# Three weight slabs instead of two beside three of a transformer block's norms

## The reference

```python
h = rms_norm(x, norm_mix[l])
proj = h @ w_in[l]                 # pool, q, k, v, the inputs of a recurrent mixer, gates
...                                # three branches from it, merged under gates
x = x + merged @ w_out[l]
x = x + conv_glu_ffn(rms_norm(x, norm_ffn[l]), ffn_up[l], ffn_conv[l], ffn_down[l])
```

## Time and profile before

| | |
|---|---|
| median of 3 runs | 2850.2 us (2846.32 to 2850.47) |
| profiled execution, device time | 2849.13 us |
| its span in the trace | 2847.3 us |
| granted TensorE clock, mean | 0.981 of full |
| TensorE busy | 2722.3 us, 96% |
| VectorE, ScalarE busy | 1810.7 us, 1119.0 us |

### The profile page before, as it was taken

One profiled execution on the slowest core, in us unless ns is written; L12 is line 12 of the kernel. 1 busy time (PEld: TensorE's weight loads), 2 busy tenths in 40 slices (PEclk: granted clock), 3 DMA queues, 4 the chain that ended last, 5 costly groups with the idle time before them and its releaser, 6 DMA issues. The chain is left out here.

```text
span 2847.3 us, 59014 instructions
## 1 busy us (share of the span) xinstructions
PE 2722.3 (96%) x25807; PEld 2489.7 (87%) x25807; DVE 1810.7 (64%) x2741; ACT 1119.0 (39%) x1818; POOL 376.0 (13%) x223
## 2 busy tenths in 40 slices
PE   8999999999999999999999999999999999899997
PEld 7988998898999998988998898999887887777785
DVE  5744345555888645834345555888637985787786
ACT  6332324523333224423324523333323343366564
POOL 0310122130111100310122130111100000010001
PEclk9999999999999999999999999999999999799999
DMA  3211222364333342211322362333322212299996
GB/s 143 76 44 34 83 82 62 118 200 171 121 133 134 121 142 91 79 37 34 94 71 73 106 191 82 119 134 135 117 91 88 94 33 74 94 411 402 381 396 252
DMA packets 115355, 380.23 MB, mean 134 GB/s; under 512 B 12800, under 2 KB 13968, under 8 KB 114704
## 3 DMA queue, kind: packets, MB, share of 16 engines
q1 hardware_dynamic: 89712, 307.18, 31.4%
q10 hardware_dynamic: 17712, 41.36, 4.0%
q0 software_dynamic: 7664, 27.82, 2.6%
HBM read 340.17 MB, written 36.13 MB: 132 GB/s over the span
## 5 line engine op out<-in xcount | busy, mean ns | idle before, releaser
L307 PE MATMUL PS<-HR,HIGHR 128*128 128x264 f32 (+1 forms) x3008 | 856.7, 285 | 1.9 <-issue 1.9
L307 PE MATMUL PS<-XR,HIGHR 128*128 128x264 f32 (+2 forms) x1792 | 564.2, 315 | 15.5 <-DVE HR L431 9.8
L307 PEld LDWEIGHTS PS<-HR,HIGHR 128*128 128x128 f32 x3008 | 570.5, 190 | 5.1 <-issue 2.1
L307 PE MATMUL PS<-XR,RINGR 128*128 128x264 f32 (+1 forms) x1600 | 456.1, 285 | 0.0
L307 PE MATMUL PS<-HH,HIGHR 128*128 128x264 f32 (+2 forms) x1504 | 436.9, 290 | 10.5 <-ACT SMALL L388 5.7
L291 ACT CAST HIGHR<-RING 128x1024 fp32r<-128x1024 f32 (+2 forms) x340 | 330.7, 977 | 265.8 <-DMA RING<-wts 117.3
L307 PE MATMUL PS<-HH,RINGR 128*128 128x264 f32 (+2 forms) x1504 | 432.1, 287 | 0.0
L302 DVE TENSOR_TENSOR RINGR<-RING,HIGHR 128x1024 fp32r<-128x1024 f32 (+2 forms) x272 | 304.9, 1125 | 163.3 <-ACT HIGHR L291 150.4
L307 PEld LDWEIGHTS PS<-XR,HIGHR 128*128 128x128 f32 x1792 | 339.9, 190 | 42.1 <-issue 12.2
L307 PE MATMUL PS<-ARENA 64*64 64x64 f32 (+7 forms) x8890 | 332.4, 234 | 29.6 <-issue 15.7
L307 PEld LDWEIGHTS PS<-ARENA 64*64 64x64 f32 (+4 forms) x8890 | 286.0, 140 | 66.1 <-issue 21.5
(11 more groups left out here) (403 smaller groups left out, 4820.0 us busy)
## 6 DMA issues: line engine op xcount, KB each, us to landing
RING<-wts SPq DMA_DIRECT2D x324, 512.0 KB, 3.6
ARENA<-wmoe SPq DMA_DIRECT2D x210, 512.0 KB, 7.4
RING<-wts SPq DMA_DIRECT2D x52, 256.0 KB, 3.0
gates<-STAGE ACTq DMA_DIRECT2D x48, 264.0 KB, 4.3
ARENA<-gates ACTq DMA_DIRECT2D x48, 264.0 KB, 3.2
ys<-RING ACTq DMA_DIRECT2D x17, 512.0 KB, 6.8
ys<-STAGE POOLq DMA_DIRECT2D x15, 512.0 KB, 11.4
RING<-wts SPq DMA_DIRECT2D x16, 384.0 KB, 3.0
```

The lines of the kernel that those rows point to most:

```text
L307: return e.matmul(out, lhsT, rhs, start=start, stop=stop, skip_group_check=True)
```

## The change

Two constants are new: `LIN_BESIDE` gives the number of slabs side by side behind the mix norm of each layer (layer 0 keeps two, layer 1 has three), and `UP_BESIDE` lists the three up slabs side by side behind the ffn norm of both layers. The calls of `high_parts` and `low_parts` that stand ahead of the norm now reach one slab further. On ScalarE that call stands behind the last square and ahead of the norm's table load; on VectorE ahead of the first scaling. The calls behind the norm stay as they are, and so do slab order and banks.

```diff
+LIN_BESIDE = (2, 3)
+UP_BESIDE = [(0, 0), (0, 1), (1, 0)]
...
-    slabs = [slab(0), slab(1)]
-    two_at = [banks.place(w, (l, "in", i), 2) for i in range(2)]
-    two = project_beside(k, e, w, slabs, k.hx, lambda q: s["part_dve"][l, "h", q], two_at, cut=True)
+    first = [slab(i) for i in range(LIN_BESIDE[l])]
+    first_at = [banks.place(w, (l, "in", i), 2) for i in range(len(first))]
+    beside = project_beside(k, e, w, first, k.hx, lambda q: s["part_dve"][l, "h", q], first_at, cut=True)
     for i in range(14):
-        if i < 2:
-            two[i].then_inc(*P.done((l, "in", i)))
+        if i < len(first):
+            beside[i].then_inc(*P.done((l, "in", i)))
...
-    high_parts(k, e, w, k.slabs.index["lin", l, 1] + 1)
+    high_parts(k, e, w, k.slabs.index["lin", l, LIN_BESIDE[l] - 1] + 1)
     rms_act(k, e, w, ("mix", l), k.rs)
...
-    low_parts(k, e, w, "lo_dve", k.slabs.index["lin", l, 1] + 1)
+    low_parts(k, e, w, "lo_dve", k.slabs.index["lin", l, LIN_BESIDE[l] - 1] + 1)
...
         if f == 0:
-            slabs = [slab(0, p) for p in range(2)]
-            at = [banks.place(w, ("up", l, 0, p), 2) for p in range(2)]
-            two = project_beside(k, e, w, slabs, rhs, lambda q: s["part_dve"][l, "f", q], at, T - t0, cut=True)
+            first = [slab(*x) for x in UP_BESIDE]
+            at = [banks.place(w, ("up", l, *x), 2) for x in UP_BESIDE]
+            beside_of = dict(zip(UP_BESIDE, project_beside(k, e, w, first, rhs, lambda q: s["part_dve"][l, "f", q], at,
+                                                           T - t0, cut=True)))
         for p in range(2):
-            if f == 0:
-                two[p].then_inc(*s["up_pe"].done((l, f, p)))
+            if (f, p) in beside_of:
+                beside_of[f, p].then_inc(*s["up_pe"].done((l, f, p)))
...
-    high_parts(k, e, w, k.slabs.index["up", l, 0, 1] + 1)
+    high_parts(k, e, w, k.slabs.index["up", l, 1, 0] + 1)
     rms_act(k, e, w, ("ffn", l), k.rs)
...
-    low_parts(k, e, w, "lo_dve", k.slabs.index["up", l, 0, 1] + 1)
+    low_parts(k, e, w, "lo_dve", k.slabs.index["up", l, 1, 0] + 1)
```

## The result

The changed kernel takes 2856.24 us in the median of 11 runs (2853.02 to 2863.87), the kernel before 2850.69 in 11 runs beside it (2845.11 to 2852.68). The ratio is 1.0025, with a 95% interval from 1.0015 to 1.0035: slower by 4 to 10 us. The forecast was 5.1 us slower, a median of 2855.3 in a range from 2850.5 to 2860.5.

What follows compares the result with a forecast made beforehand. TensorE, busy 2722.3 of 2847.3 us, was taken as the bound. A loss of 1.8 us without the clock plus 3.3 from it made 5.1 slower: 2854.2 profiled, median 2855.3, range 2850.5 to 2860.5.

Steps and rivals of the forecast that it cites:

- The clock's term: Half-clock falls behind the new stalls: likeliest two of three stages, mix among them, 1.6 + 1.7 = 3.3 us lost.
- one sign that was named for being wrong: Across the three stages: the clock falling at none or all of them would show the prediction wrong.
- The split ahead of the norm: ScalarE's copy between last square and table load lengthens the norm by 0.9 us, 0.45 in layer 1's mix norm.
- Three slabs fill the gaps: Behind the norms TensorE runs 144 matmuls without a gap; three slabs end 3.6, 2.9 and 2.0 us earlier, 8.4 in sum.
- The stall ahead of (1,1): Up stages: TensorE idles some 2.7 us for (1,1)'s low part; 0.6 us won in layer 0, 0.2 lost in layer 1.
- the worst case: Layer 1 up stage: three slabs end later, (1,1) at 1776.85 instead of 1775.85 us.
- The mix stage: Layer 1's mix stage: lin 3 starts 2.2 us later without the clock, a clock fall adds 1.7.
- the sign to look for: Layer 1's mix stage in the new trace: lin 3 starts 31.5 us instead of 29.7 behind the first matmul.
- The chain named: Mix stage on ScalarE: lin 0's end, tanh, lin 1's copy, split, square, then lin 2's copy, 2.2 us later.
- The gain of 8 us without new waits: Rival for all three stages: (1,1) and tanh ready when three slabs end, 8.4 us faster, 2841.8; chance 0.07.
- The held clock: Rival: clock holds behind the up stalls, falls at most briefly in the mix stage; 1.8 us slower, 2852.0; chance 0.2.
- The third rival: Clock falls behind all three stages and stays low as long as behind a norm; 10.2 us slower, 2860.4; chance 0.13.

Runs made afterwards that it cites:

- e6: Kernel before, two slabs side by side, with only the third slab's split made ahead of the three norms; ratio 1.0005.
- e4: Changed kernel plus high and low part of (1,1) made right behind the normed tiles in both up stages; ratio 1.0002.
- e10: Changed kernel run once more, unaltered, in another session; ratio to the kernel before 1.0018.
- e1: Changed kernel with three slabs behind layer 1's mix norm alone, both up stages back to two; ratio to the kernel before 1.0008.
- e8: Changed kernel with ScalarE reordered in layer 1's mix stage: lin 2's copy behind lin 1's, lin 3's split and the square among the sigmoids, lin 4's split after; ratio 1.0029.
- e7: Changed kernel with 20 unread matmuls put into TensorE's wait ahead of (1,1) in both up stages; ratio to the kernel before 1.0014.
- e5: Changed kernel, mix back to two slabs; up stages: third split before last square, (1,1) split behind normed tiles, (2,0) split one step sooner; 2843.89 against 2851.59 us before.
- e2: Changed kernel with three slabs behind both ffn norms, mix norm back to two; ratio to the kernel before 1.0005.

## Why the prediction was right

Sign and cause were right, and the total lies in the range. The clock's term was too small, and one sign that was named for being wrong did show; point by point:

- *The split ahead of the norm.* Put at 0.9, 0.45 and 0.9 us. e6 measures 0.94, 0.57, 0.94; in the changed kernel's profile the first matmul is 1.1 late in the up stages (5.8 against 4.7) and 0.57 in the mix stage. A little small.
- *Three slabs fill the gaps.* Right: no wait between first matmul and stall. What filling is worth, if nothing comes behind, was put at 8.4 us for all three stages with the split's cost paid. e4's (1,1) starts 3.9 and 1.9 us sooner than before, where 3.6 and 2.9 were put.
- *The stall ahead of (1,1).* Put at 2.7 us in both, and (1,1) at 0.6 sooner and 0.2 later. Measured 2.60 and 2.55, 0.4 sooner and 1.1 later in the first profile (0.0 and 1.2 in e10). The 1.1 is the one term at the edge: the slow stretch behind layer 1's norm, which I let end when it ended before, moved and grew. I had this as the worst case, 1 us.
- *The mix stage.* Put at 2.2 us later without the clock and 3.9 with it; measured 3.3 to 3.5 at lin 3, and 3.1 still there at lin 5 (e1). In the sign to look for, lin 3 stood at 31.5 us behind the first matmul, without the clock; it measures 32.4. The chain named was the right one: the wait for tanh is 1.65 (1.7 forecast), one for the copy of lin 2 is there (1.07), the first sigmoid starts 1.9 later than before, and e8 takes the 3 us at lin 3 away by ScalarE's order. I was right that VectorE gives nothing back.
- *The clock.* Falls put at two chances in three with 1.6 us each, so 1.1 in the mean; measured eight in ten and 1.5 in the mean. In both profiles of the changed kernel (after, e10) it fell in all three stages, not two. The prediction had named a fall "at none or all of them" as a sign of being wrong: what was wrong is the size of this term, and not that the stalls drop the clock, as e7 shows. By the Trainium skill's advice on pauses ("TensorE: Matmul & The Clock Gate", section "Why this matters for your kernels") the clock would have held at this length; the measurement differs in eight of ten stalls and decides. e7 shows that the pause of 2.6 us is what drops it.
- *Rivals.* The gain of 8 us without new waits is ruled out for this change, and e5 shows where it lies: 7.7 us from the two up stages alone, once the three splits come in time. The held clock is ruled out as the usual case. The third rival, falls as long as behind a norm, happened in single stages (2.9 and 2.8 us), not in all.
- *Sum.* 5.1 put; the medians differ by 5.55, the ratios say 7.1 (4.3 to 10) and 5.1 (2.3 to 7.7). It came out around the bound of 0.2% (0.25% and 0.18%). Two terms were small: the clock by some 0.4 us a stall, the slow stretch behind layer 1's norm by 0.9. By stage lengths the miss is larger than by the ratios: the two up stages were put at 1.2 together and measure 4.2 in the mean of after, e2 and e10, the mix stage was put at 3.9 and measures 3.4. That 5.1 is so near the ratio of e10 is in part luck.

What stays open: why the clock held behind two of ten stalls of the same length, and the miss of e8's ratio. No run has the mix stage with three slabs and both ScalarE's and VectorE's splits in time, so what three slabs are worth there at best isn't shown.

## What to carry to other kernels

Slabs that run side by side also end side by side: what followed the last of them was covered by it until now, and must be ready at its end. So when more work is put beside a slow producer, move the preparation of the next two steps along with it, into the producer's own idle time, and put work "in advance" ahead of the last instruction of the critical chain, not behind it. A stage whose next step hangs on the result of the first slab, as tanh and the sigmoids do here, wants that slab early. A third beside it delays it (the copy of lin 0 by 3.1 us), and what ScalarE has queued behind it adds to that.

## What the runs showed of the hardware

A pause of TensorE of 2.55 to 2.60 us, after 15 us of full work, brought the granted clock from 1.00 to 0.50 in eight of ten cases, and the next slab of 5.8 us then took 1.4 to 2.9 us longer; 20 matmuls without use in the pause (2.57 us) kept it at 1.00 in both stages. The length of the pause doesn't tell the two kinds apart: the two that held were 2.59 and 2.60 us. I had expected falls less often.

Several short pauses did it too. In layer 1's mix stage with three slabs TensorE waits some 1.65, 1.05 and 1.8 us within 8 us, and behind the second or third of these waits the clock fell to 0.50 in all six profiles with ScalarE's old order, for 3.4 or 6.8 us. With waits of 1.65, 0.67 and 0.38 us at that place (e8), or one of 1.56 (before), it stayed at 1.00.
